# A two-layer decoder trunk with 32 experts a layer on one core: the expert stage without its lag of one expert

## The reference

```python
x = x + y_mixers @ w_out
h = rmsnorm(x, moe_norm)
# group = argmax of 4, then the best 2 of its 8 experts
# for every expert e, on the rows sent to it:
y = (silu(xb @ w1[e]) * (xb @ w3[e])) @ w2[e]      # 1024 -> 512 -> 1024
x = x + sum of the two y's, each times its gate
```

## Time and profile before

| | us |
|---|---|
| median of three runs | 1745.98 |
| lowest and highest | 1740.31, 1749.12 |
| the profiled execution | 1741.77 |
| its span in the trace | 1739.9 |
| PE busy | 1643.3 (94%) |
| DVE busy | 960.7 (55%) |
| ACT busy | 454.8 (26%) |
| mean granted clock of PE | 0.983 |

### The profile page before, as it was taken

The page is one execution under the profiler, slowest core; times in us unless marked ns, Lnnn a source line. Parts: engine busy times, 40 slices in busy tenths (PEclk is TensorE's granted clock), DMA queues, the critical chain, the costliest instruction groups (busy, mean ns, idle before and its releaser), DMA issues. The chain is left out here.

```text
span 1739.9 us, 27655 instructions
## 1 busy us (share of the span) xinstructions
PE 1643.3 (94%) x11194; PEld 886.4 (51%) x11323; DVE 960.7 (55%) x1665; ACT 454.8 (26%) x777; POOL 156.4 (9%) x188
## 2 busy tenths in 40 slices
PE   8999878899999999999998999999999999999996
PEld 6756667665633333333334977665633333333332
DVE  4548576551346666666657322561336666666666
ACT  4353444362211111111113221462211111111112
POOL 2002524310100000000000040120100000000000
PEclk9999999999999999999999999999899999999998
DMA  6441000028699999999994250209599999999993
GB/s 201 116 127 55 7 3 4 12 89 346 224 422 425 424 425 426 424 426 426 425 423 164 89 178 24 98 2 363 205 422 425 426 426 425 426 425 426 426 421 129
DMA packets 103409, 475.42 MB, mean 273 GB/s; under 512 B 29041, under 2 KB 67953, under 8 KB 76656
## 3 DMA queue, kind: packets, MB, share of 16 engines
q1 hardware_dynamic: 99904, 461.03, 65.7%
q0 software_dynamic: 3376, 12.58, 1.9%
HBM read 454.71 MB, written 18.87 MB: 272 GB/s over the span
## 5 line engine op out<-in xcount | busy, mean ns | idle before, releaser
L855 DVE SCALAR_TENSOR_TENSOR x<-ps,gate_by_expert,x 128x512 f32<-128x512 f32 x512 | 348.2, 743 | 309.3 <-PE ps L810 309.1
L751 PE MATMUL ps<-w_unit,xT 128*48 128x512 f32 x1024 | 452.8, 595 | 14.0 <-DMA w_unit<-in_moe_w 13.9
L752 PE MATMUL ps<-w_unit,xT 128*48 128x512 f32 x1024 | 453.1, 595 | 0.0
L751 PEld LDWEIGHTS ps<-w_unit,xT 128*48 128x48 f32 x1024 | 125.0, 123 | 318.6 <-issue 318.5
L788 PE MATMUL ps<-w_unit,hidT 128*48 128x512 f32 x1024 | 245.8, 600 | 2.1 <-issue 1.9
L810 PE MATMUL ps<-y_high_low,slots_to_tokens 128*128 128x512 f32 x512 | 156.9, 426 | 6.6 <-DVE x L855 5.9
L880 ACT ACTIVATE y_high_low<-ps 48x512 fp32r<-48x512 f32 x128 | 75.8, 592 | 317.0 <-PE ps L788 304.2
L810 PEld LDWEIGHTS ps<-y_high_low,slots_to_tokens 128*128 128x128 f32 x512 | 86.4, 189 | 124.4 <-issue 57.7
L1332 PE MATMUL ps<-hT_high,w_high 128*128 128x512 f32 (+1 forms) x336 | 135.6, 404 | 6.3 <-PE ps L1334 3.9
L873 ACT ACTIVATE gate_act_hid<-ps 48x512 f32<-48x512 f32 x64 | 37.9, 592 | 384.2 <-PE ps L752 384.2
L1334 PE MATMUL ps<-hT_high,w_low 128*128 128x512 f32 (+1 forms) x336 | 132.9, 395 | 0.0
(11 more groups left out here) (371 smaller groups left out, 1941.2 us busy)
## 6 DMA issues: line engine op xcount, KB each, us to landing
w_unit<-in_moe_w SPq DMA_DIRECT2D x176, 2048.0 KB, 31.4
w_unit<-in_moe_w SPq DMA_DIRECT2D x32, 1024.0 KB, 22.0
x_rows<-sorted_rows SPq DMA_DIRECT2D x64, 192.0 KB, 26.7
w_unit<-in_od_w_qkv SPq DMA_DIRECT2D x12, 1024.0 KB, 5.4
w_raw<-in_ev_w_in SPq DMA_DIRECT2D x10, 1024.0 KB, 6.0
sorted_rows<-bias SPq DMA_DIRECT2D x32, 192.0 KB, 5.6
w_unit<-in_ev_w_out SPq DMA_DIRECT2D x2, 2048.0 KB, 10.8
w_unit<-in_od_w_out SPq DMA_DIRECT2D x2, 2048.0 KB, 11.8
```

The costliest lines, as they stand in the source:

```text
L751: nc.tensor.matmul(ps_up(n)[0:MB, :], xT[b][:, k, :], w1[:, k, :], start=k == 0, stop=k == KD - 1)
L752: last = nc.tensor.matmul(ps_up(n)[UP:UP + MB, :], xT[b][:, k, :], w3[:, k, :], start=k == 0, stop=k == KD - 1)
L855: nc.vector.scalar_tensor_tensor(out=xs, in0=ps_c[i % 4][:, :], scalar=gate(t), in1=xs, op0=ALU.mult, op1=ALU.add).then_inc(added, 1)
```

## The change

With `OWN = 1`, all loops over `range(1, OWN)` are empty. PE's turn n becomes: up(n), first half of spread(n-1), turn_hidden(n), turn_rows(n+1), down(n) with the second half of spread(n-1) in its middle. Expert 0's down product comes before expert 1's up product and has nothing in its middle. DVE's turn becomes: split_low(n-1), select(n), hidden(n), gain_rows(n+1), and then all eight adds of n-1. ACT's turn: split_high(n-1), silu(n), copy_hidden(n). Pieces are taken in the plain order (n,0), (n,1), (n,2). Expert 0, not 31, uses `ps_x` for its down product. In the router, SP loads unit 9 in front of the wait for the scattering and of the rows.

```diff
+            sp.wait_ge(out_done, 2 * TT)
+            wts.load(sp, GUEST[1:])
             for j in range(2):
                 sp.wait_ge(scattered[j], 16 * TT)
             for n in range(SLOTS):
                 r.load_rows(sp, xrows, n, n * CAP)
-            sp.wait_ge(out_done, 2 * TT)
-            wts.load(sp, GUEST[1:])
...
-LAST = N_EXP - 1
+LAST, OWN = N_EXP - 1, 1
...
-    for n in range(1, N_EXP):
+    for n in range(1, OWN):
         pieces += [(n, 0), (n, 1), (n - 1, 2)]
-    return pieces + [(LAST, 2)]
+    pieces += [(OWN - 1, 2)]
+    for n in range(OWN, N_EXP):
+        pieces += [(n, 0), (n, 1), (n, 2)]
+    return pieces
...
-    ps_y = lambda n: ps_x if isinstance(n, int) and n == LAST else ps[2]
+    ps_y = lambda n: ps_x if isinstance(n, int) and n == OWN - 1 else ps[2]
...
-        if isinstance(n, int) and n == LAST:
-            pe.wait_ge(xT_out, N_EXP)
+        if isinstance(n, int) and n == OWN - 1:
+            pe.wait_ge(xT_out, OWN + 1)
...
# PE
-            for n in range(1, N_EXP):
-                up_expert(pe, n, n - 2)
-                turn_hidden(pe, n - 1)
+            turn_hidden(pe, OWN - 1)
+            wts.arrived(pe, OWN - 1, 2)
+            down(pe, OWN - 1, wts.view(OWN - 1, 2), lambda ts: spread(pe, OWN - 2, range(TT // 2)))
+            spread(pe, OWN - 2, range(TT // 2, TT))
+            for n in range(OWN, N_EXP):
+                up_expert(pe, n, n - 1)
+                turn_hidden(pe, n)
                 if n < LAST:
                     turn_rows(pe, slot(n + 1), use(n + 1))
-                down_expert(pe, n - 1, n - 2)
-            turn_hidden(pe, LAST)
-            wts.arrived(pe, LAST, 2)
-            down(pe, LAST, wts.view(LAST, 2), lambda ts: spread(pe, LAST - 1, range(TT // 2)))
-            spread(pe, LAST - 1, range(TT // 2, TT))
-            keep_warm(nc, c, ps_h, 30)
+                down_expert(pe, n, n - 1)
+            keep_warm(nc, c, ps_x, 44)
             spread(pe, LAST, range(TT))
-            keep_warm(nc, c, ps_h, 20)
+            keep_warm(nc, c, ps_x, 20)
...
# DVE
-            split_low(dve, LAST - 1)
-            select(dve, LAST, slot_rows(LAST))
-            add(dve, LAST - 1, early, gate_of(LAST - 1))
+            for n in range(OWN - 2, LAST):
+                if n >= 0:
+                    split_low(dve, n)
+                select(dve, n + 1, slot_rows(n + 1))
+                if n >= OWN - 1:
+                    hidden(dve, n + 1, n + 1)
+                    if n + 2 <= LAST:
+                        gain_rows(dve, n + 2, n % 2)
+                if n >= 0:
+                    add(dve, n, range(GROUPS), gate_of(n))
             split_low(dve, LAST)
-            add(dve, LAST - 1, late, gate_of(LAST - 1))
             add(dve, LAST, range(GROUPS), gate_of(LAST))
...
# ACT
+            for n in range(OWN, N_EXP):
+                split_high(act, n - 1)
+                silu(act, n)
+                copy_hidden(act, n)
```

More of the change, by code:

```diff
@@ L955, in _ @@
             up_expert(pe, 0, -1)
-            for n in range(1, N_EXP):
+            for n in range(1, OWN):
                 up_expert(pe, n, n - 2)
                 turn_hidden(pe, n - 1)
+                turn_rows(pe, slot(n + 1), use(n + 1))
+                down_expert(pe, n - 1, n - 2)
+            turn_hidden(pe, OWN - 1)
[5 more added lines that the diff above has]
+                turn_hidden(pe, n)
                 if n < LAST:
                     turn_rows(pe, slot(n + 1), use(n + 1))
-                down_expert(pe, n - 1, n - 2)
-            turn_hidden(pe, LAST)
-            wts.arrived(pe, LAST, 2)
-            down(pe, LAST, wts.view(LAST, 2), lambda ts: spread(pe, LAST - 1, range(TT // 2)))
-            spread(pe, LAST - 1, range(TT // 2, TT))
-            keep_warm(nc, c, ps_h, 30)
+                down_expert(pe, n, n - 1)
+            keep_warm(nc, c, ps_x, 44)
             spread(pe, LAST, range(TT))
-            keep_warm(nc, c, ps_h, 20)
+            keep_warm(nc, c, ps_x, 20)
             def more(e, b, m):
@@ L1009, in _ @@
                 hidden(dve, n, n)
-                if n < LAST:
-                    gain_rows(dve, n + 1, (n + 1) % 2)
+                gain_rows(dve, n + 1, (n + 1) % 2)
                 select(dve, n - 1, slot_rows(n - 1))
@@ L1052, in _ @@
                 copy_hidden(act, n - 1)
-            copy_hidden(act, LAST)
-            split_high(act, LAST - 1)
+            copy_hidden(act, OWN - 1)
+            if OWN >= 2:
+                split_high(act, OWN - 2)
+            for n in range(OWN, N_EXP):
+                split_high(act, n - 1)
+                silu(act, n)
+                copy_hidden(act, n)
             split_high(act, LAST)
```

## The result

| | before | after |
|---|---|---|
| median, us | 1743.14 (4 runs) | 1815.29 (4 runs) |
| profiled execution, us | 1741.77 | 1815.55 |
| its span, us | 1739.9 | 1813.7 |
| mean granted clock of PE | 0.983 | 0.991 |

The ratio is 1.0419, 95% interval 1.0397 to 1.0442: 72 us slower between the medians, 73.8 between the spans. The prediction was 1820, slower, by 74.2; of the 4.7 us between 1820 and 1815.29, 2.8 are the median of before, which stood at 1746.0 when the prediction was made.

What follows compares the result with a forecast made beforehand. PE's own work was taken to bound the expert stages, with DMA almost as slow. Stages of +44.9 and +47.4 less two tails of 9.05 gave +74.2, so 1820 us; 8 in 10 within 1792 to 1850.

Steps and rivals of the forecast that it cites:

- The bound: Expert stages: PE's own work sets the 13.98 us turn; DMA is nearly as slow, 15.27 us an expert, helped by 11 prefilled units.
- First wait: Each turn, PE's transposes wait for this expert's silu and product, starting at S+1.47 instead of S+1.02: +0.45 us.
- Second wait: Each turn, DVE's adds stand behind gain_rows, so the second half of the spread waits for banks: +1.12 us.
- The turn: One expert's turn in the expert stages: 13.98 + 1.57 = 15.55 us, between 15.1 and 16.15.
- A stage: First to last silu of each expert stage: 13.2 plus 30 turns, 479.7 us, so +44.9 and +47.4.
- Tail: Last silu to last add: 16.0 us instead of 25.05, as one down product is left; -9.05 us a stage.
- Sum: Whole kernel: 44.9 + 47.4 - 2 x 9.05 = +74.2 us, giving 1820 us against the median.
- Rival 1: PE's clock falls after idle gaps in the turns: 1846 us if one turn in four, 1925 if every turn; chance 0.09.
- Rival 2: DVE's adds free the banks in time, so a turn is 14.43 us: 1753 us, no change; chance 0.05.
- Rival 3: DMA becomes the bound through one 2 us idle gap a turn: up to +13 us a stage, 1846 us; chance 0.05.
- Unit 9, its value: Router: loading this weight unit before the scattering ends gains nothing, as PE isn't waiting for weights.
- Unit 9, its price: Router: the early load overlaps the scattering; taken as 0, at worst +2.5 us a layer.

Runs made afterwards that it cites:

- adds in front: Against the kernel after, VectorE does the first four adds of the expert before directly behind hidden, in front of gain_rows; 1757.49 us, 1.010 of before.
- half the bytes: Against the kernel after, each whole-unit weight transfer behind the first 11 pieces brings only half its unit; 1813.28 us, turns 15.52 and 15.53 us.

## Why the prediction was right

- **The bound.** PE's own work set the turn of 13.98 and DMA was almost as slow. Right: more idle time on PE showed in full, and the waits for weights went to nothing.
- **First wait, +0.45.** Measured +0.53 to 0.54. The estimate of the hand-over from `hidden` to the transposes, 0.15, is 0.17 in the trace; the rest is that `hidden` starts 0.10 after the silu's end (607.11 + 0.59 to 607.80) and not 0.03. Shown by taking the silu out of the chain: 15.00.
- **Second wait, +1.12.** Measured +1.01: both parts of the spread's second half start within 0.08 of the times worked out (4.77 and 6.10 against 4.71 and 6.02). Shown twice, by adds in front without the lag and by adds behind with it.
- **The turn, 15.55.** 15.52; the two errors nearly cancel.
- **A stage, +44.9 and +47.4.** +44.1 and +48.3. The 30 turns gave 0.8 us less in each stage than predicted (0.03 each). The other term that was off is the first turn, 13.2 in both: it was 13.23 in the first stage and 14.92 in the second. Expert 0 has no spread to cover `hidden`; its transposes waited 1.52 us in either stage:

```profile
1306.58 0.68 PE L780 MATMUL ps<-ident,gate_act_hid 48*128 48x48 f32 x4 [1.52 <-DVE gate_act_hid L826]
```

and in the second the granted clock fell just behind:

```profile
1305.00:1310.00 5.00, 3.01 (x14) 1.44 (x15) 1.80 (x3) 0.92 (x2) 0.00 (x0) 0.88 0.98 367
1310.00:1315.00 5.00, 5.00 (x20) 1.77 (x18) 1.25 (x2) 1.18 (x2) 0.00 (x0) 0.78 0.78 315
```

- **Tail, -9.05.** -9.1 in both stages.
- **Sum.** 44.1 + 48.3 - 18.2 = 74.2, as predicted, against 73.8 between the spans; -0.4 lies outside the two stages. That it agrees to the tenth is luck: the 60 turns gave 1.7 less than predicted, the fallen clock of the second stage 1.7 more.
- **Rival 1, the clock.** Wrong for the turns: with idle gaps of 0.45 to 0.53 and 0.58 us in each, none of the 60 changed its length. Right once, at expert 0 of the second stage, for 1.7 us. The Trainium skill (TensorE: Matmul & The Clock Gate, A second HAM failure mode: psum-queue depth-cycling) has the clock swing in a kernel that pauses between groups while it cycles through PSUM banks; this trace has two such pauses in each turn and holds 1.00 from 600 to 700 us.
- **Rival 2, no second wait.** Out; the run with the adds in front shows what it would have been, 1.0% slower and not within 0.5%. Its turn is 14.52 and not 14.43, since the first wait is larger than I took it (5 us), and its first turns are 14.93 us and not 13.2 (3.5 us).
- **Rival 3, DMA.** Out by half the bytes.
- **Unit 9, its value.** Nothing, as predicted: in the changed kernel PE waits for no weights. In the kernel before it is worth 0.3%, which the prediction didn't say.
- **Unit 9, its price.** Taken as 0, which the trace doesn't bear out, though it is small. The last scattering transfers and the rows asked for behind them, before and after:

```profile
469.33 0.96 POOL L579 DMA_INDIRECT sorted_rows<-xn,dest  x1 [0.30 <-issue]
```

```profile
458.01 0.96 POOL L579 DMA_INDIRECT sorted_rows<-xn,dest  x1 [7.30 <-DVE dest L510]
...
466.39 0.96 POOL L579 DMA_INDIRECT sorted_rows<-xn,dest  x1 [0.30 <-issue]
...
471.99 1.28 SPq L1105 DMA_DIRECT2D x_rows<-sorted_rows  x3
```

From the last issue to the rows it was 3.57 us before (472.90 - 469.33) and is 5.60 now; in the second router it was 4.2 and is 6.2. The packets of the trace show where it starts: those issued at 458.01 ran from 462.79 on, 4.8 us later, toward the end of the load, whose packets ran from 457.13 to 466.36; before it was 1.5 us (459.90 to 461.43). No packet of the scattering ran from 457.83 to 462.79, so there the two did not share the engines packet by packet; whether the load kept them off or they were ready late isn't shown. Measured from the end of `w_out`, the rows were asked 1.0 us later than before in the first router and 0.4 earlier in the second, where PE of the kernel before had run at the lower clock for 6.8 us. No run takes this price alone; it is within the 2.5 us a layer that the prediction set as its worst case.

## What to carry to other kernels

Before taking a lag out of a written-out order, walk the chain that it covered (here silu, product, transposes) and then every list that the new order changes: the work that was pushed behind a waiting instruction cost twice as much as the chain itself (1.01 against 0.53 us a turn), and moving four adds gave some 55 of the 72 us back. A lag is also not free at the end, where it leaves a product over; keep it while PE is the bound and drop it where the transfers would make PE wait anyway. When two resources are both full, halve one's work and see whether the time moves.

## What was not expected of the hardware

An idle gap of 1.52 us of PE at expert 0 was followed by the lower clock in one stage of the kernel after (first turn 14.92 us) and not in the other (13.23 us), with the same instructions. The other runs say the same: behind the same gap of 1.52 us it fell in both stages with the adds in front and in the second alone with half the bytes; behind one of 0.90 us it fell in one of four stages (the two runs without the wait for the silu). So the length of the gap alone doesn't tell it. Gaps of 0.45 to 0.58 us in every turn never were followed by it, in 60 turns.

A small transfer of 192 KB in a full queue waits for what stands before it: one 2 MB unit more in front of it brought the rows of expert 31 late by 1.19 us in one stage and by 3.85 us in the other. There the clock was low too, and the turn took 6.2 us more than with the rows in front (28.06 against 21.90), 2.3 of it beyond the wait. And beside a load of 2 MB the scattering transfers of another queue started 4.8 us behind their issue, where it was 1.5 us without it.
